# Stick-breaking attention in a three-layer block: suffix sums in the log domain by matmul, or a running product of sigmoids

## What is computed

```python
z = einsum('bqhd,bshd->bhqs', qb, k_b) * scale
strict = key_pos < t                        # keys before the query
log_1mb = where(strict, log_sigmoid(-z), 0)
after = cumsum(log_1mb, axis=keys, reverse=True) - log_1mb
att = where(strict, exp(log_sigmoid(z) + after), 0)
ob = einsum('bhqs,bshd->bqhd', att, v_b)
```

## Time and profile before

| | us |
|---|---|
| median of 3 runs | 1563.7 (1562.65 to 1565.59) |
| span of the profiled execution | 1560.3 |
| PE busy | 1520.5 (97%) |
| DVE, ACT, POOL busy | 868.7, 631.5, 611.3 |
| stick stage, 1001.6 to 1105.5 | 103.9 |

### The profile page before, as it was taken

One profiled execution on the slowest core, in us unless ns is written; L12 is line 12 of the kernel. 1 busy time (PEld: TensorE's weight loads), 2 busy tenths in 40 slices (PEclk: granted clock), 3 DMA queues, 4 the chain that ended last, 5 costly groups with the idle time before them and its releaser, 6 DMA issues.

```text
span 1560.3 us, 22590 instructions
## 1 busy us (share of the span) xinstructions
PE 1520.5 (97%) x9097; PEld 1204.2 (77%) x9097; DVE 868.7 (56%) x1567; ACT 631.5 (40%) x1140; POOL 611.3 (39%) x452
## 2 busy tenths in 40 slices
PE   7999999999999999999999999999999999999997
PEld 6887666887888788887877766766787888888886
DVE  4895656136874467338169995577476322333224
ACT  6323566354323366453343335654544322222222
POOL 6454211444454213444325242212364455444451
PEclk9999999999999999999999999999999999999999
DMA  9485100234532211242213221101232232232321
GB/s 359 138 295 176 41 28 28 81 121 176 210 114 84 71 42 57 82 149 81 100 29 107 88 81 55 55 27 55 74 130 81 96 107 95 95 108 81 108 86 76
DMA packets 86215, 158.66 MB, mean 102 GB/s; under 512 B 2736, under 2 KB 20704, under 8 KB 86112
## 3 DMA queue, kind: packets, MB, share of 16 engines
q1 hardware_dynamic: 82256, 148.91, 28.6%
q10 hardware_dynamic: 3856, 8.32, 1.5%
HBM read 155.10 MB, written 2.12 MB: 101 GB/s over the span
## 4 chain that ended last, share of the span: by engine, by line
PE 77%; DVE 17%; ACT 2%; DMA 2%; issue 1%; POOL 1%; DVEq 0%; SPq 0%; ACTq 0%
PE banks L477 10%; PE banks L478 10%; PE banks L479 10%; PE banks L473 7%; PE banks L474 7%; PE banks L475 7%; PE banks L592 4%; PE banks L594 3%; PE banks L593 3%; PE banks L615 2%; PE banks L630 2%; PE banks L640 2%; DVE slots L1997 2%; DVE max L1995 2%; DVE work_lo L1750 2%; DVE ev L1750 2%
## 5 line engine op out<-in xcount | busy, mean ns | idle before, releaser
L451 POOL TENSOR_TENSOR w_lo<-w_raw,w_hi 128x512 fp32r<-128x512 f32 x440 | 597.8, 1393 | 911.9 <-ACT w_hi L1048 834.1
L1048 ACT ACTIVATE w_hi<-w_raw 128x2048 fp32r<-128x2048 f32 (+1 forms) x112 | 210.9, 1883 | 202.3 <-DMA w_raw<-w_ff_dram 141.5
L473 PE MATMUL banks<-xh,w_hi 128*128 128x512 f32 x640 | 250.3, 391 | 0.0
L474 PE MATMUL banks<-xl,w_hi 128*128 128x512 f32 x640 | 249.0, 389 | 0.0
L475 PE MATMUL banks<-xh,w_lo 128*128 128x512 f32 x640 | 249.0, 389 | 0.0
L477 PE MATMUL banks<-w_hi,xh 128*128 128x512 f32 x384 | 153.1, 399 | 10.9 <-POOL w_lo L445 9.7
L478 PE MATMUL banks<-w_lo,xh 128*128 128x512 f32 x384 | 150.8, 393 | 0.0
L479 PE MATMUL banks<-w_hi,xl 128*128 128x512 f32 x384 | 150.7, 393 | 0.0
L477 PE MATMUL banks<-w_hi,yh 128*128 128x512 f32 x384 | 150.1, 391 | 0.3 <-DVE yl L1881 0.2
L478 PE MATMUL banks<-w_lo,yh 128*128 128x512 f32 x384 | 149.5, 389 | 0.0
L479 PE MATMUL banks<-w_hi,yl 128*128 128x512 f32 x384 | 149.5, 389 | 0.0
(11 more groups left out here) (335 smaller groups left out, 2541.0 us busy)
## 6 DMA issues: line engine op xcount, KB each, us to landing
w_raw<-w_ff_dram SPq DMA_DIRECT2D x32, 1024.0 KB, 5.3
w_raw<-w_in_dram SPq DMA_DIRECT2D x22, 1024.0 KB, 5.1
work_hi<-w_ada_dram SPq DMA_DIRECT2D x16, 1024.0 KB, 6.8
w_raw<-rec_w_in_dram SPq DMA_DIRECT2D x16, 1024.0 KB, 5.4
w_raw<-att_w_in_dram SPq DMA_DIRECT2D x14, 1024.0 KB, 5.9
work_lo<-w_ada_dram SPq DMA_DIRECT2D x8, 1024.0 KB, 8.0
w_raw<-ple_w_gate_dram SPq DMA_DIRECT2D x8, 1024.0 KB, 5.0
w_raw<-att_w_out_dram SPq DMA_DIRECT2D x4, 1024.0 KB, 5.1
```

What stands on the lines that cost most here:

```text
L451: ins = pool.tensor_tensor(wlo[s][:, k, :], raw[s][:, k, :], wh[s][:, k, :].bitcast(F32), ALU.subtract)
L473: pe.matmul(out, w_h, x_h, start=start, stop=False)
L474: pe.matmul(out, w_h, x_l, start=False, stop=False)
L1048: act.activation(wh[s][:, 0:kn, :], raw[s][:, 0:kn, :], ACT.Copy).then_inc(w_split, 1)
```

## The change

The stage now has queries on partitions, like the top attention, and runs in 12 steps (`STK_STEPS`): four pairs, and for each three steps, with key widths 256+128 (query blocks 1 and 0 together), 384 and 512. For each step:
- PE computes z once (`stick_scores`); DVE adds the mask to the diagonal blocks (`stick_mask`); ACT takes sigmoid(z) into `stk_att` and sigmoid(-z) into `stk_rest` (`stick_sigmoid`).
- DVE turns each row of `stk_rest` into a running product from the last key backward, in place, by a scan whose operands have a step of -1, and multiplies `stk_att` with it, shifted by one key (`stick_products`).
- PE transposes the weights (`stick_turns`) into banks 4 and 5, ACT copies them to `stk_turned`, PE multiplies with the values (`stick_output`) in 128x128 products.

The second scores, the triangle and ones matmuls, and the logs, exponentials and splits on DVE are gone. The gate tiles leave bank 7 by ACT (`gates_moved`). The scores of the first two steps stand in the last but one step of the top attention, and the table of sigmoid is loaded there. The constant loaded is a 128x128 mask instead of 128x512.

```diff
-STK_UNIT = [(0, 0), (1, 0), (2, 0), (2, 256)]
-STK_COLS = [512, 384, 384]
-STK_DENSE = [(8, 0, 2, 1, 3, 2), (0, 3, 3, 2, 4, 4), (0, 3, 3, 2, 4, 4), (0, 3, 3, 2, 8, 0)]
+STK_STEPS = 12
+STK_ROWS = [[(1, 0), (0, 256)], [(2, 0)], [(3, 0)]]
+STK_COLS = [384, 384, 512]
+STK_DIAG = [128, 256, 384]
+STK_AHEAD = 5
+STK_DENSE = [(1, 2), (3, 2), (2, 1)] + 3 * [(4, 4), (3, 2), (2, 1)]
...
+            def stick_scores(t):
+                i, r = divmod(t, 3)
+                if t >= 2:
+                    pe.wait_ge(sg("stk_sigmoids"), 2 * (t - 1))
+                for q, c in STK_ROWS[r]:
+                    for e in range(2):
+                        hs = slice(HD * e, HD * e + HD)
+                        mm = pe.matmul(ps[:, 2 * (t % 2) + e, c:c + (q + 1) * P], feat["D"][hs, i, q * P:q * P + P],
+                                       feat["D"][hs, 4 + i, 0:(q + 1) * P], start=True, stop=True)
...
+            def stick_turns(t):
+                pe.wait_ge(sg("stk_att"), t + 1)
+                for e in range(2):
+                    for c in range(0, STK_COLS[t % 3], P):
+                        tr = pe.transpose(ps[:, 4 + e, c:c + P], stk_att[t % 3][:, e, c:c + P], ident[:, :])
+                tr.then_inc(sg("stk_turned"), 1)
+            def stick_output(t):
+                i, r = divmod(t, 3)
+                if r == 0:
+                    pe.wait_ge(*((sg("top_out"), 4) if i == 0 else (sg("stk_out"), i)))
+                pe.wait_ge(sg("stk_moved"), t + 1)
+                for q, c in STK_ROWS[r]:
+                    for j in range(q + 1):
+                        for e in range(2):
...
-            def stick_sums(i, j):
-                pe.wait_ge(sg("stk_sp"), stk(i, 1, STK_UNIT[j][0]))
-                stick_scores(i, j, False)
-                for e in range(2):
-                    for j2 in range(j, TT):
...
-                        pe.matmul(unit_bank(e, j, j2), tri if j2 == j else ones, stk_hi[e][u][:, cut], start=False, stop=False)
-                        mm = pe.matmul(unit_bank(e, j, j2), tri if j2 == j else ones, stk_lo[e][u][:, cut], start=False, stop=j2 == TT - 1)
...
+            stick_beside(STK_AHEAD)
+            for t in range(STK_STEPS):
+                if t > 0:
+                    stick_output(t - 1)
+                if t + 2 < STK_STEPS:
+                    stick_scores(t + 2)
+                stick_beside(STK_DENSE[t][0])
+                stick_turns(t)
+                stick_beside(STK_DENSE[t][1])
+            stick_output(STK_STEPS - 1)
...
+            act.sem_inc(sg("gb2_free"), 1)
+            act.wait_ge(sg("top_summed"), 16)
+            stick_sigmoid(0, False)
+            stick_sigmoid(1, True)
+            stick_sigmoid(1, False)
...
+            for t in range(STK_STEPS):
+                if t > 0:
+                    gates_moved(tiles_done(t - 2) if t > 1 else 0, tiles_done(t - 1))
+                if t + 2 < STK_STEPS:
+                    stick_sigmoid(t + 2, True)
+                    stick_sigmoid(t + 2, False)
+                w = STK_COLS[t % 3]
+                act.wait_ge(sg("stk_turned"), t + 1)
+                act.activation(stk_turned[:, :, 0:w], ps[:, 4:6, 0:w], ACT.Copy).then_inc(sg("stk_moved"), 1)
+                if t % 3 == 2:
+                    high_after("gb2", t // 3)
+            gates_moved(tiles_done(STK_STEPS - 2), KT)
...
+            def stick_products(t):
+                w, rest = STK_COLS[t % 3], stk_rest[t % 2]
+                dve.wait_ge(sg("stk_sigmoids"), 2 * t + 2)
                 for e in range(2):
+                    for q, c in STK_ROWS[t % 3]:
+                        n = (q + 1) * P
+                        x = rest[:, e, c:c + n]
+                        x = bass.AP(x.tensor, x.offset + n - 1, [x.ap[0], [-1, n]])
+                        V.mark(dve.tensor_tensor_scan(x, x, x, 1.0, ALU.mult, ALU.bypass))
+                V.wait()
+                att = stk_att[t % 3][:, :, 0:w - 1]
+                dve.tensor_tensor(att, att, rest[:, :, 1:w], ALU.mult).then_inc(sg("stk_att"), 1)
...
+            stick_products(0)
+            for t in range(STK_STEPS):
+                if t + 2 < STK_STEPS:
+                    stick_mask(t + 2)
+                if t > 0 and t % 3 == 0:
+                    stick_split(t // 3 - 1)
+                if t + 1 < STK_STEPS:
+                    stick_products(t + 1)
```

More of the change, by code:

```diff
@@ L75, with tiles_done @@
 SLOTS = 3
-def stk(i, e, u):
-    return 6 * i + 2 * (2 - u) + e + 1
+def tiles_done(step):
+    return (STK_AHEAD + sum(a + b for a, b in STK_DENSE[:step + 1])) // KT
 def gate_bank(l, m):
@@ L601, in all_banks_free, with attention @@
                     pe.wait_ge(*emptied(n))
-            def attention(x, pairs, bias, side, probs, turned, q_of, k_of, v_of):
+            def attention(x, pairs, bias, side, probs, turned, q_of, k_of, v_of, ahead=None):
                 steps, per = 4 * pairs, pairs // 2
@@ L631, in attention @@
                             mm.then_inc(sg(x + "_turned"), 1)
+                    if ahead and t == steps + 1:
+                        ahead()
                     if t >= 3:
@@ L940, in stick_beside @@
-            def stick_beside(i, block):
-                first = sum(STK_DENSE[i][:block])
-                for unit in range(first, first + STK_DENSE[i][block]):
-                    beside("gb2", 2 * i + unit // 8, unit % 8)
-            def stick_output(i):
-                if i > 0:
-                    pe.wait_ge(sg("stk_out"), i)
-                for j in range(TT):
-                    for e in range(2):
-                        hs, v0 = slice(HD * e, HD * e + HD), G + i * P + HD * e
-                        u, o = STK_UNIT[j]
-                        pe.wait_ge(sg("stk_att"), stk(i, e, u))
-                        mm = pe.matmul(ps[hs, 6, j * P:T], tok["C"][:, j, v0:v0 + HD], stk_at[e][u][:, o:o + (TT - j) * P],
-                                       start=j == 0, stop=j == TT - 1)
-                mm.then_inc(sg("stk_o"), 1)
@@ new lines, in _, with stick_beside, first_scores @@
+            dense = [0]
+            def stick_beside(units):
+                for _ in range(units):
+                    beside("gb2", *divmod(dense[0], KT))
+                    dense[0] += 1
+            def first_scores():
+                stick_scores(0)
+                stick_scores(1)
+            attention("top", 4, False, "ga2", top_s, top_p, lambda i: feat["B"][:, i, :], lambda i: feat["B"][:, 4 + i, :],
+                      lambda j, hd: tok["C"][:, j, HD * hd:HD * hd + HD], ahead=first_scores)
@@ L1422, in stick_weights, with gates_moved @@
-            def stick_weights(i, u):
-                w = STK_COLS[u]
-                for e in range(2):
-                    act.wait_ge(sg("stk_arg"), stk(i, e, u))
-                    act.activation(stk_at[e][u][:, 0:w], ps[:, 3 * e + u, 0:w], ACT.Exp).then_inc(sg("stk_att"), 1)
-            for u in (2, 1, 0):
-                stick_logs(0, u)
-            for i in range(4):
-                stick_weights(i, 2)
-                stick_weights(i, 1)
-                if i < 3:
-                    stick_logs(i + 1, 2)
-                stick_weights(i, 0)
-                if i < 3:
-                    stick_logs(i + 1, 1)
-                high_after("gb2", i)
-                if i < 3:
-                    stick_logs(i + 1, 0)
+            def gates_moved(first, last):
+                for tile in range(first, last):
+                    i, second = divmod(tile, 2)
+                    beside("gb2", tile, ev[:, second, :] if i == 0 else feat["D"][:, i - 1 + 4 * second, :])
```

163 lines of the change are left out of this document (45 added, 118 removed).

## The result

| | before | after |
|---|---|---|
| median, us | 1563.2 (1560.3 to 1565.6, 4 runs) | 1538.1 (1536.3 to 1539.4, 4 runs) |
| ratio | | 0.9844, 95% interval 0.983 to 0.9859 |
| span of the profiled execution | 1560.3 | 1537.4 |
| PE busy | 1520.5 | 1495.9 |
| stage frame (below) | 108.9 | 85.0 |

The change makes the kernel 25 us faster (interval 22 to 27). The forecast was 1543.8 us, 19.9 us less, in a range that began at 1539.5: the direction came out as forecast, and so did what bounds the stage, but the time lies 1.4 us under the range. The step that failed is the price of a pair of heads on PE: 19.9 us forecast, 19.2 measured. In the rows of after, the first answers to the earlier trace rows, the second is PE's recorded waits in the stage, for the earlier trace rows, and the third is the stage itself, with the columns of the earlier trace rows.

What follows compares the result with a forecast made beforehand. PE was taken to bound the kernel. PE work saved, 23.9 us, less 4.0 us of new waits gave 19.9 us off 1563.7, so 1543.8 us; the range was 1539.5 to 1551.5 us.

Steps and rivals of the forecast that it cites:

- The price of a pair: PE work per pair of heads in the changed stage, taken from the top attention: 19.9 us, bounds 19.4 and 20.5.
- Only the grouping differs: Stage against top attention, per pair: fewer fp32 groups save 0.5 us, six dense blocks instead of four add 0.4 us.
- Waits, 4.0 us: New PE waits in the stage, mainly for ACT's copies and gate tile moves: 4.0 us in all, bounds 0 and 12.
- Output behind one unit: In every third step PE waits for ACT's copy of the transposed weights before the output: 0.5 us, four times.
- Gate tile: PE waits for ACT to clear bank 7 before the next dense tile: free at 3.85 us, 0.35 us wait, three times.
- Start: At the stage's beginning ACT's queue delays the first copy: 0.5 us late, taken as 1.0 us with hand-overs.
- Scans backward at the forward price: DVE's running products cost the forward scan's 2.07 ns an element; bounds were that time and twice it.
- Hidden: DVE's 12.6 us a pair, in about 20.9, runs a step ahead of the transposes, so PE never waits for it.
- Clock: PE's clock stays full in the stage; the rival, a fall to 1.2 GHz from many short waits, had chance 0.03.
- Nothing changes behind the stage: After the stage only the time of day changes; POOL supplies merge2's chunks in about 5 us, needed every 11 us.
- PE groups much longer than the attention's: A listed sign that the forecast was wrong: PE groups in the stage lasting much longer than in the top attention.
- DVE and ACT work that goes is worth nothing by itself: In the old stage PE was busy 102.8 of 103.9 us, so removing DVE or ACT work alone saves nothing.

Runs made afterwards that it cites:

- two units, gate tile first: The changed kernel with two dense units behind every third step's transposes and the gate tile moved ahead of ACT's rounding of a weight chunk: 1533.7 us, repeated 1533.8.
- the other two comparisons: The changed kernel run again, unaltered, each time against the kernel before on the same chip: 1537.6 against 1560.5 us, and 1536.6 against 1560.9 us.
- without the sums: The kernel before without its triangle and ones matmuls, second scores and the rest of the old pipeline kept: 1543.0 us, ratio 0.9883, frame 92.3 us.
- that with two dense units: The changed kernel with two dense units instead of one behind the transposes of every third step: 1534.1 us, ratio 0.9828.
- the top attention's transposes apart: The changed kernel with the top attention's transposes moved from between scores and output into the middle of the dense units: 1536.7 us, ratio 0.9839.

## Why the prediction was off, step by step

**The price of a pair, step "19.9 us each".** This step failed. It divided 59.68 us between the scores at 930.19 and 989.87 by three. The scores in between are here:

```profile
950.54 1.13 PE L615 MATMUL banks<-slots 64*128 64x512 f32 x4
...
970.90 1.13 PE L615 MATMUL banks<-slots 64*128 64x512 f32 x4
```

The pairs last 20.35, 20.36 and 18.97 us. The last holds two dense units less (42 dense matmuls instead of 48). The comparable pair is 20.35, so the step read 0.45 us a pair too little.

**"Only the grouping differs", -0.5 and +0.4.** This step failed by more, the other way. A pair here needs 19.2, 1.15 us less than the attention's. I had counted a start-up of 0.15 us for each group that goes. What the transposes pay for their neighbours, the largest term, was not in it. Read from the starts, the twenty transposes cost 0.57 + 0.57 + 0.79 = 1.93 us here, and 0.37 + 0.58 + 0.81 + 1.03 = 2.79 us in the attention: 0.86 less, of which 0.15 is the group that goes and 0.7 the neighbours (0.24 in each of three groups). One output group less (0.15) and one group of scores less (0.2) make 1.2. So the -0.5 was right. The +0.4 for six dense blocks instead of four was not: by starts the blocks of a pair take 11.87 us here (two units, gate tile first) and 11.82 in the attention, 0.05 more, since a block that ends at transposes pays nothing on exit. The saving on PE was 4 x (25.87 - 19.2) = 26.7 us, not 23.9, above the bound of 25.9. The two errors had opposite signs, and that the forecast came within 6 us is partly luck: with the pair read rightly and the grouping as forecast, the forecast would have been 1545.6, farther off.

**Waits, 4.0 us.** The mechanism was right in each, the sum a quarter too large. Output behind one unit: forecast 1.33 us after the transposes, measured 1.36 (1019.48 to 1020.84); the wait is 0.50 by starts (0.42 in the bracket), as forecast, four times: 2.0 us. Gate tile: forecast free at 3.85 us, measured 3.59 (1023.07), wait 0.2, not 0.35, three times: 0.6 us. Start: 0.47 in the bracket and 0.54 by starts, not 1.0. The sum is 3.1 us.

**DVE.** Scans backward at the forward price: right. Hidden: right. Its work was 53.5 us, 13.4 a pair against 12.6. POOL's lock-out is in it, 0.9 us for a multiplication and 1.6 for two scans in each of three pairs by the rows above; the rule of the Trainium skill, page "SBUF — State Buffer", section "SBUF: two separate sides", that the prediction names agrees with the 1.86 against 0.96 us. **Clock:** right. **Nothing changes behind the stage:** right, but for a wait under *Open*.

**Sum.** 26.7 - 3.1 = 23.6 us against 23.9 in the frame; the forecast's 23.9 - 4.0 was 19.9. Of the 4.0 us of error 2.8 are the price of the pair and 0.9 the waits. Of the 5.7 us between 1543.8 and 1538.1, 4.0 are the stage; 0.5 is the base (the forecast began at 1563.7, and the median of before with one more run is 1563.2, in later batches 1560.5 to 1561.4); the last 1.2 is put down to scatter, as the other two comparisons give 22.9 and 24.3 us. The range was too narrow because its lower end came from bounds of steps that I took for known; "PE groups much longer than the attention's" was listed as what would be wrong, and shorter was not.

**"DVE and ACT work that goes is worth nothing by itself."** True of before, yet incomplete. With about the same PE work (19.9 us a pair) and the old DVE work, the frame stood at 92.3. Of the 7.3 us between that and 85.0, PE's work explains 4 x (19.9 - 19.2) = 2.8. The other 4 to 5 of the change's 24 us came from what the change did beside PE, which keeps a PE that has become faster from waiting: the lighter DVE, and the gate tiles that ACT moves instead of DVE. No run separates these two. As more than half of the waiting without the sums is for gate tiles, moving only those to ACT in the old kernel is an obvious rival, and it is untested.

**Open.** One wait of 2.2 us for POOL behind the stage (PE L977) stands in two of the changed kernel's three traces and in that with two dense units; it is 0.7 us with the top attention's transposes apart and none in the others. So it doesn't belong to the change alone. POOL's block there took 8.38 us instead of 7.27, so an estimate of its cost is 1 us. Its cause was not tried.

## What to carry to other kernels

A price taken from a similar stage is only good if every period of it is looked at: print the starts of all periods, and count the instructions in each before dividing. On a PE-bound stage the order of groups has a price of its own: put full-array transposes between full-array matmuls where their result still comes in time, and two dense units rather than one where a result goes to ACT and back. Read a short wait by starts, too: brackets were 0.08 us short or missed it. Before trusting a saving on the bounding engine, look at what its next waits would be for: with 24 us less PE work alone the old pipeline gave only 16.6.

## What the hardware showed that was not expected

- The same six fp32 transposes take 0.57 us between 128x512 dense matmuls and 0.75 to 0.81 us ahead of an output that uses half the array's columns; eight take 0.79 against 0.97 and 1.03.
- What a wait does to PE's clock varied. One of 3.3 us was followed by some 3.3 us at 1.2 GHz (half of it, 1.7 us, lost), and in a stage with waits of 12 us in all some 14 us ran at that clock. The same waits of 1.9 and 0.3 us were followed by a stretch at 0.67 in one execution of the changed kernel and by the full clock in another. Five waits of half a us brought no fall.
- A scan whose operands run backward in memory takes 1206 ns for 512 elements, forward 1221.
